# The turn back of the S5 states moved from GpSimd to VectorE, in a two-layer hybrid encoder kernel

## What is computed

```python
proj = x @ w_in
dq, dk, dv, mq, mk, mv, mo, mi, mf, su = split_columns(proj, IN_WIDTHS)
# S5: 16 groups, each with a 64-dim complex diagonal state
bu = jnp.einsum('bsgc,gpc->bsgp', uf.astype(jnp.complex64), b_bar)
a_seq = jnp.broadcast_to(lam_bar, (s_,) + lam_bar.shape)[None]
_, states = lax.associative_scan(combine, (a_seq, bu), axis=1)
y = jnp.einsum('bsgp,gcp->bsgc', states, c_mat).real + d_skip * uf
```

## Time and profile before

| what | us |
|---|---|
| median of 3 runs | 1382.65 (1382.14 to 1382.77) |
| profiled execution, its own time | 1379.54 |
| its span in the trace | 1377.7 |
| TensorE busy | 1263.9 (92%) |
| VectorE busy | 826.5 (60%) |
| ScalarE busy | 577.2 (42%) |
| GpSimd busy | 184.0 (13%) |

### The profile page before, as it was taken

The page is one execution under the profiler, slowest core; times in us unless marked ns, Lnnn a source line. Parts: engine busy times, 40 slices in busy tenths (PEclk is TensorE's granted clock), DMA queues, the critical chain, the costliest instruction groups (busy, mean ns, idle before and its releaser), DMA issues.

```text
span 1377.7 us, 15974 instructions
## 1 busy us (share of the span) xinstructions
PE 1263.9 (92%) x6568; PEld 1069.3 (78%) x6568; DVE 826.5 (60%) x1218; ACT 577.2 (42%) x656; POOL 184.0 (13%) x172
## 2 busy tenths in 40 slices
PE   6999999989769999999999999999875898899996
PEld 5788888878658888888887888888763786688885
DVE  5577556593676565554565786566846746544554
ACT  4444444425433545444444444444163344344441
POOL 1018000382000000000000170003810000000000
PEclk9999999999789999999999999999976999899999
DMA  8655555433134355555546555554211434355550
GB/s 288 229 183 187 187 177 176 136 117 123 34 104 162 128 185 193 192 193 186 183 168 243 183 188 188 175 180 137 81 62 61 166 110 153 122 187 194 192 191 31
DMA packets 155912, 219.53 MB, mean 159 GB/s; under 512 B 6816, under 2 KB 127776, under 8 KB 155840
## 3 DMA queue, kind: packets, MB, share of 16 engines
q1 hardware_dynamic: 152448, 205.61, 44.6%
q0 software_dynamic: 3120, 11.85, 2.4%
q10 hardware_dynamic: 272, 1.05, 0.2%
HBM read 217.44 MB, written 1.05 MB: 159 GB/s over the span
## 4 chain that ended last, share of the span: by engine, by line
PE 78%; DVE 12%; ACT 3%; issue 3%; POOL 2%; DMA 2%; SPq 0%; DVEq 0%; POOLq 0%
PE PS L466 24%; PE PS L468 23%; PE PS L467 23%; DVE WL L1373 3%; DMA RAW<-in_ffn_w_up 2%; PE PS L497 1%; ACT WH L1040 1%; DVE COUT L1557 1%; DVE ZS L1545 1%; PE PS L534 1%; PE PS L961 1%; PE PS L985 1%; ACT XH L1040 1%; POOL RO L1994 1%; ACT PR L1157 1%
## 5 line engine op out<-in xcount | busy, mean ns | idle before, releaser
L1373 DVE TENSOR_TENSOR WL<-RAW,WH 128x2048 fp32r<-128x2048 f32 (+1 forms) x198 | 445.7, 2255 | 266.9 <-ACT WH L1040 266.8
L1040 ACT ACTIVATE WH<-RAW 128x2048 fp32r<-128x2048 f32 (+1 forms) x198 | 370.3, 1876 | 151.5 <-DMA RAW<-in_ffn_w_up 132.0
L466 PE MATMUL PS<-WH,XH 128*128 128x512 f32 x832 | 334.1, 402 | 24.8 <-DVE WL L1373 9.3
L467 PE MATMUL PS<-WL,XH 128*128 128x512 f32 x832 | 328.1, 394 | 0.0
L468 PE MATMUL PS<-WH,XL 128*128 128x512 f32 x832 | 327.9, 394 | 0.0
L466 PEld LDWEIGHTS PS<-WH,XH 128*128 128x128 f32 x832 | 158.4, 190 | 59.0 <-issue 10.0
L468 PEld LDWEIGHTS PS<-WH,XL 128*128 128x128 f32 x832 | 158.3, 190 | 33.6
L467 PEld LDWEIGHTS PS<-WL,XH 128*128 128x128 f32 x832 | 158.7, 191 | 31.0
L466 PE MATMUL PS<-WH,HH 128*128 128x512 f32 x352 | 138.7, 394 | 5.9 <-issue 5.9
L468 PE MATMUL PS<-WH,HL 128*128 128x512 f32 x352 | 137.7, 391 | 0.0
L467 PE MATMUL PS<-WL,HH 128*128 128x512 f32 x352 | 137.7, 391 | 0.0
(11 more groups left out here) (310 smaller groups left out, 1761.9 us busy)
## 6 DMA issues: line engine op xcount, KB each, us to landing
RAW<-in_ffn_w_gate SPq DMA_DIRECT2D x88, 512.0 KB, 3.7
RAW<-in_ffn_w_up SPq DMA_DIRECT2D x88, 512.0 KB, 4.7
RAW<-in_ffn_w_down SPq DMA_DIRECT2D x88, 512.0 KB, 4.3
RAW<-in_w_in SPq DMA_DIRECT2D x44, 512.0 KB, 4.4
RAW<-in_xattn_wkv SPq DMA_DIRECT2D x32, 512.0 KB, 4.1
RAW<-in_xattn_wq SPq DMA_DIRECT2D x16, 512.0 KB, 4.4
RAW<-in_w_out SPq DMA_DIRECT2D x12, 512.0 KB, 3.9
RAW<-in_xattn_wo SPq DMA_DIRECT2D x12, 512.0 KB, 4.3
```

What stands on the lines that cost most here:

```text
L466: nc.tensor.matmul(out_ap, sh, mh, start=first, stop=False)
L467: nc.tensor.matmul(out_ap, sh, ml, start=False, stop=False)
L1040: return nc.scalar.activation(dst, src, ACT.Copy)
L1373: return v.tensor_tensor(dst, full, hi.bitcast(F32), ALU.subtract)
```

## The change

The function `turn_back` is taken out of GpSimd's program and put, with the same four instructions on the same operands, into VectorE's. There it stands right behind `s5_turn_in` of the same pair. Both waits of the function are kept. The counts of links (waits of an engine on its own last result) follow.

```diff
-DVE_LINKS, POOL_LINKS = 219, 52
+DVE_LINKS, POOL_LINKS = 223, 48
...
+            def turn_back(l, j):
+                dve.wait_ge(z_ready.sem, z_ready.at(l, j + 1))
+                if j >= 2:
+                    dve.wait_ge(state_used.sem, state_used.at(l, j - 1))
...
+                v.tensor_tensor(x, z, cos, ALU.mult)
+                link(v.tensor_tensor(z, z, sin, ALU.mult))
+                v.tensor_tensor(x[:, 0, :], x[:, 0, :], z[:, 1, :], ALU.subtract)
+                v.tensor_tensor(x[:, 1, :], x[:, 1, :], z[:, 0, :], ALU.add).then_inc(state_ready.sem, 1)
...
                 conv(l, 0)
                 split()
                 s5_turn_in(l, 0)
+                turn_back(l, 0)
                 split()
                 conv(l, 1)
                 s5_turn_in(l, 1)
+                turn_back(l, 1)
                 split()
                 s5_turn_in(l, 2)
+                turn_back(l, 2)
                 split()
                 s5_turn_in(l, 3)
+                turn_back(l, 3)
                 gates_out(l)
...
                 rope(l, 0, 0)
                 rope(l, 0, 1)
-                turn_back(l, 0)
-                turn_back(l, 1)
                 rope(l, 1, 0)
-                turn_back(l, 2)
                 rope(l, 1, 1)
-                turn_back(l, 3)
                 gate_scale(l)
```

More of the change, by code:

```diff
@@ L1547, in s5_turn_in @@
                 z.then_inc(z_ready.sem, 1)
+            def turn_back(l, j):
+                dve.wait_ge(z_ready.sem, z_ready.at(l, j + 1))
+                if j >= 2:
+                    dve.wait_ge(state_used.sem, state_used.at(l, j - 1))
+                z = ZS[:, j % 2]
+                x = ZX[:, j % 2]
+                cos = EC[:, 2 * j:2 * j + 2, :].rearrange("p f k -> p (f k)").unsqueeze(1).to_broadcast([P, 2, SEQ])
+                sin = ESN[:, 2 * j:2 * j + 2, :].rearrange("p f k -> p (f k)").unsqueeze(1).to_broadcast([P, 2, SEQ])
+                v.tensor_tensor(x, z, cos, ALU.mult)
+                link(v.tensor_tensor(z, z, sin, ALU.mult))
+                v.tensor_tensor(x[:, 0, :], x[:, 0, :], z[:, 1, :], ALU.subtract)
+                v.tensor_tensor(x[:, 1, :], x[:, 1, :], z[:, 0, :], ALU.add).then_inc(state_ready.sem, 1)
             def conv(l, half):
@@ L2001, in rope @@
                     ins.then_inc(roped.sem, 1)
[L2003 to L2015, removed]
             def gate_scale(l):
```

## The result

The changed kernel takes **1417.33 us** (median of 4 runs, 1416.67 to 1419.02) against 1382.39 in runs of the kernel before on the same chip: a ratio of 1.0259, 95% interval 1.0247 to 1.0271. That is 34.9 us more; the forecast was 34.8 more. The profiled execution took 1419.02 us with a span of 1417.2.

A forecast was written before the change was run, and what follows sets the result against it. VectorE's list was taken to bound the stretch before MM1. Delay 13.0 plus clock 5.6 us in the first layer, 13.0 plus 3.2 in the second, made 34.8 over the median 1382.65: 1417.4 us, range 1401 to 1427.

The forecast's parts named there:

- What bounds: In the stretch before MM1, VectorE's list was named the bound; TensorE's only wait reaching 1 us there was 4.7 us.
- The turn back, 2.1 us each: The four instructions added to VectorE's list: 2.1 us for each turn back, 8.4 us for four.
- Rope beside VectorE, 5.0 us: GpSimd's 12 keys' rope instructions meeting VectorE's work before DV1: ten times 0.5 us, between 0 and 8.8.
- DV1: TensorE's job whose split ends later: start at 288.85 instead of 283.09, a new gap of 5.8 us.
- The serial chain: From DV1's start to MM1, TensorE and VectorE wait in turn without overlap: 28.3 us, MM1 13.0 us later.
- The clock, 8.8 us new: Low clock behind new gaps at DV1 and MM0: 2.81 us each in the first layer, 1.61 in the second.
- The sum: First layer 18.6 us, second 16.2: 34.8 us more, giving 1417.4 us.
- Rival 1: Serial chain as forecast, but no low clock at DV1 and MM0: 8.8 us less, 1408.6; chance 0.08.
- Rival 2: Only occupancy counts, waits always met: MM1's split moves 3.2 us a layer, 6.4 in all, 1389.1; chance 0.05.
- Rival 3: Before MM1, releasing GpSimd outweighs the work added to VectorE: 3.8 us faster, 1378.9; chance 0.03.

The follow-up runs named there:

- e6: Changed kernel with turn backs 2 and 3 moved behind the split of MM1 in VectorE's list, waits kept: 1381.57 us, ratio 1.0006.
- e7: Changed kernel with turn backs 0 and 1 behind DV1's split, 2, 3 and gates behind MM1's, keys' rope held until after turn in 3: 1371.08 us.
- e8: Kernel before with only the gates moved behind the split of MM1, turn backs still on GpSimd: 1385.48 us, ratio 1.0027.
- e5: Changed kernel with own buffers for pairs 2 and 3, so the waits for state_used are gone: 1384.11 us, ratio 1.0013.
- e11: Kernel before, turn backs on GpSimd, with VectorE waiting for state_used ahead of MM0's split and the gates: 1398.39 us, ratio 1.0118.
- e3: Changed kernel with extra matmuls, used by nothing, filling TensorE's three gaps in each layer: 1407.49 us, ratio 1.0175.
- e1: Changed kernel with turn backs 2 and 3 put back on GpSimd, 0 and 1 kept on VectorE: 1388.07 us, ratio 1.0031.
- e9: Changed kernel with the keys' two rope halves on GpSimd placed where VectorE idles, behind turn in 2 and turn in 3: 1406.10 us, ratio 1.0175.
- e12: e7 without its hold on rope, so the keys' rope starts as soon as its data are there: 1378.31 us, ratio 0.9965.
- e2: Kernel before with turn backs 2 and 3 moved to VectorE, 0 and 1 left on GpSimd: 1409.67 us, ratio 1.0191.
- e4: Changed kernel with the keys' rope on GpSimd held until VectorE has read the input products of pair 2: 1409.04 us, ratio 1.0185.

## Why the prediction was right

- **What bounds.** VectorE's list ahead of each split, not occupancy: e6 and e7 show it, since they keep all the instructions and lose the loss.
- **The turn back, 2.1 us each.** Measured 2.01 undisturbed (301.53 to 303.54). The second, which rope meets, took 3.84 (283.57 to 287.41).
- **Rope beside VectorE, 5.0 us.** Held. In the changed kernel conv(1) was stretched by 0.7 us, turn in 1 by 1.8, turn back 1 by 1.8 and the split of DV1 by 0.6 (2.84 for 2.28): 4.9. It was expected ahead of the split and lay partly in it. The mean price held, 0.5 us for ten meetings, or 0.4 for all twelve instructions. By the rule of the Trainium skill (SBUF — State Buffer, "Who interferes with whom") by which the engine that issues first has the ports for its whole instruction, taken alone as one instruction for each meeting, the term would have been 8.8. The other side of the lock, a GpSimd instruction held up through whole VectorE instructions, is what e8 shows, with 5.11 us for 0.72.
- **DV1.** A gap of 5.8 us was forecast, 5.62 measured. For MM0 it was 4.4 and 4.54, for MM1 7.5 and 7.41, in both layers.
- **The serial chain.** 28.3 us from DV1 to MM1 without the clock. Measured from 290.30 to 323.84 it is 33.54; less the low clock in it, 2.24 at DV1 and 2.87 at MM0, that is 28.4. That the waits make the chain is shown by e5 (waits away) and e11 (waits alone).
- **The clock, 8.8 us new.** DV1 took 2.24 and 2.62 us more, and MM0 2.87 and 1.47, together 9.2; e3, which takes the low clock away, puts the new share at 8.5 to 9.9. I had put 2.81 on each job of the first layer and 1.61 on each of the second. For MM0 that was near; for DV1 it was 0.6 too much in the first layer and 1.0 too little in the second, so that part of the sum was right by luck.
- **The sum.** 18.6 and 16.2 us forecast, 17.9 and 17.4 measured in the S5 stretch. The second layer was 1.2 us worse, by DV1's clock. Behind it the mLSTM stretch took back nothing in the first layer and 0.7 us in the second. The two profiled spans differ by 39.5 us, 4 more than the two S5 stretches, and that difference lies outside them; the medians, 34.9 apart, don't have it (the profiled execution of the kernel before, 1379.54, was faster than each of its four runs, and that of the changed one, 1419.02, was the slowest of its four).
- **Rival 1**, the clock holds, stood at 1408.6. e3 makes that case, but at MM1 too, and took 1407.49.
- **Rival 2**, occupancy alone, had the size of 1389.1; e5 is that case and took 1384.1. The list moved by 2.6 us (3.2 in the working), but I had left the low clock at MM1 as it was, and added the gap at MM1. In e5 the gap moves to DV1 and MM1's clock stays up, which pays for it.
- **Rival 3**, faster since GpSimd is the slower engine. The rule of the Trainium skill (GPSIMD Engine Reference, section 4.1) is right about the work and silent about the queue: the same instructions on VectorE gave a ratio of 1.0259 in one order and 0.9924 in another, with rope held back in the latter too.

## What to carry to other kernels

Before moving a step to another engine, list with each of its waits what is queued behind it there: a wait that held up nobody on an engine with slack becomes a wait of everyone on the engine that feeds TensorE. Put what feeds the bound first and the moved step behind it, as late as its reader allows (e6, e7), or give it a buffer so that it need not wait (e5). And price work and waits together: alone they cost about 2 and 16 us here, together 35.

## What was not expected of the hardware

- **A fall of the clock without idle time.** In nine of the twelve experiments, e8 among them, the granted clock fell for some microseconds in one layer right behind the input products of the first pair and the gate matmuls, though TensorE was busy throughout. e8, stretches of the first layer, and one 256-column matmul before and one after the fall:

```profile
253.00:257.00 4.00, 4.00 (x29) 3.04 (x29) 0.57 (x2) 2.40 (x2) 0.00 (x0) 1.00 0.62 185
257.00:261.00 4.00, 4.00 (x23) 4.00 (x22) 3.86 (x7) 0.00 (x0) 0.00 (x0) 0.57 0.22 81
```

```profile
256.77 0.28 PE L466 MATMUL PS<-XH,WH 128*128 128x256 f32 x1
...
259.63 0.41 PE L466 MATMUL PS<-XH,WH 128*128 128x256 f32 x1
```

  What TensorE had done just before was narrow: matmuls that read 32 partitions, and then four that read 8 and write 4. The traces of before, after, e1, e9 and e12 have the same work there and no fall in either layer, so what decides it stays open. A second such fall lies in the mLSTM stretch of the first layer of e2, e3, e4, e9, e11 and e12, behind eight matmuls that read 4 partitions: in e11 the granted clock is 0.50 from 336.3 to 338.3 us with TensorE busy, and that stretch takes 1.5 us more than before. The same work stands there in every kernel. The rows price the first fall: one 256-column matmul of e8 follows the other after 0.12 us at the full clock and after 0.21 at the low one, which over the 16 from 257.27 to 260.48 is 1.4 us.
- **The same gap, two clocks.** A gap of 3.05 us before MM0 left the clock at 1.00 in one layer of e12 and was followed by 0.50 in the other. So a low clock behind a gap of that size is a likelihood, and a price of 1.6 to 2.8 us for it is a bound and not a term.
- **The lock lasts over instructions in a row.** GpSimd's instructions of 0.72 us took 5.11 and 5.33 us beside two splits (4.47 us in e8), and in e1 7.31 beside three (6.68 us). VectorE left no opening for it between splits, while its own instructions were stretched by 0.4 to 0.5 us a meeting on average. The kernel before shows it already, in a rope instruction beside the splits that start at 301.85; there nobody waited for it:

```profile
301.82 7.29 POOL L1994 TENSOR_TENSOR RO<-RO,PW 128x256 f32<-128x256 f32 x1 [0.18 <-POOL PW L1993]
```
